# Loading the first block of input weights in two column halves, ahead of the buffer clears, in a two-layer decoder trunk

## What is computed

```python
def even_layer(h, w_in, conv_w, pool_w, pool_scale, w_out):
    xa, gb, gc, za, xp, zp = split(h @ w_in)              # six parts of 512 columns
    ya = short_gated_conv(xa, gb, gc, conv_w) * silu(za)  # gb * conv3(gc * xa)
    yb = multiscale_pool(xp, pool_w, pool_scale) * silu(zp)
    return concatenate([ya, yb], axis=-1) @ w_out

def odd_layer(h, w_in, ln_g, ln_b, w_s, b_s, w_out):
    u, v, z = split(h @ w_in, 3)                          # 1024 columns each
    v = layernorm(v, ln_g, ln_b)
    sv = tril(w_s) applied over chunks of 128 positions, per head, plus b_s
    return (u * sv * silu(z)) @ w_out

for i in range(2):
    h = rmsnorm(x, pre_norm[i])
    m = even_layer(h, ...) if i == 0 else odd_layer(h, ...)
    x = x + rmsnorm(m, post_norm[i])
```

## Time and profile before

| | us |
|---|---|
| median of 3 runs | 1076.64 |
| lowest, highest | 1073.21, 1088.56 |
| the profiled execution, its time | 1074.72 |
| its span on the slowest core (core 4) | 1073.2 |
| spans of the other seven | 1063.5 to 1069.7 |
| PE busy in the span | 978.3 |
| DVE, POOL, ACT busy | 691.9, 467.0, 385.5 |

### The profile page before, as it was taken

The page is one execution under the profiler, slowest core; times in us unless marked ns, Lnnn a source line. Parts: engine busy times, 40 slices in busy tenths (PEclk is TensorE's granted clock), DMA queues, the critical chain, the costliest instruction groups (busy, mean ns, idle before and its releaser), DMA issues.

```text
span 1073.2 us, 26957 instructions; the slowest of 8 cores (1063.5 to 1073.2 us)
## 1 busy us (share of the span) xinstructions
PE 978.3 (91%) x9144; PEld 857.3 (80%) x9144; DVE 691.9 (64%) x1826; ACT 385.5 (36%) x908; POOL 467.0 (44%) x703
## 2 busy tenths in 40 slices
PE   0879989999899999999999998999999999999994
PEld 0758878888788887878888887888888878887883
DVE  1565766658766664776666587666658657667651
ACT  3232524433433433343344234334432334324331
POOL 3223634454443545444344544434454444534452
PEclk9899999999999999999999999999999999999996
DMA  9999700222000022200002220000222000210011
GB/s 223 184 163 165 108 2 2 80 80 80 2 2 2 2 80 80 79 2 2 2 2 80 80 80 1 2 2 2 80 80 80 2 2 2 80 41 2 1 41 40
DMA packets 18328, 54.61 MB, mean 51 GB/s; under 512 B 1024, under 2 KB 1408, under 8 KB 18064
## 3 DMA queue, kind: packets, MB, share of 16 engines
q0 software_dynamic: 8592, 16.91, 10.5%
q1 hardware_dynamic: 9600, 35.98, 9.2%
HBM read 53.01 MB, written 16.78 MB: 65 GB/s over the span
## 4 chain that ended last, share of the span: by engine, by line
PE 62%; DVE 11%; POOL 8%; issue 7%; DMA 7%; ACT 4%; DVEq 0%; POOLq 0%; ACTq 0%; SPq 0%
PE psG L285 39%; PE psO L285 21%; DVE tmp L285 6%; POOL xres L285 5%; DMA Win<-win 4%; ACT tmp L285 2%; PE psT L285 2%; DVE small L285 2%; DMA xres<-x 2%; POOL small L285 2%; DMA out<-xres 1%; ACT xs L285 1%; DVE yT L285 1%; DVE pooled L285 1%; DVE hbuf L285 1%
## 5 line engine op out<-in xcount | busy, mean ns | idle before, releaser
L285 PE MATMUL psG<-hT,Win 128*128 128x256 bf16 x5120 | 602.7, 274 | 22.5 <-DVE yT L285 7.0
L285 PEld LDWEIGHTS psG<-hT,Win 128*128 128x128 bf16 x5120 | 493.1, 98 | 88.7 <-issue 30.5
L285 ACT ACTIVATE tmp<-psG 128x256 f32<-128x256 f32 (+1 forms) x324 | 121.8, 380 | 367.5 <-PE psG L285 201.3
L285 PE MATMUL psO<-Wout,yT 128*128 128x256 bf16 x2048 | 240.5, 276 | 12.4 <-DVE tmp L285 5.6
L285 PEld LDWEIGHTS psO<-Wout,yT 128*128 128x128 bf16 x2048 | 200.5, 99 | 39.5 <-issue 14.4
L285 POOL TENSOR_TENSOR yT<-tmp 128x256 bf16<-128x256 f32 x192 | 140.5, 734 | 198.6 <-DVE tmp L285 176.4
L285 POOL TENSOR_TENSOR xres<-xres,tmp 128x256 f32<-128x256 f32 x256 | 189.1, 739 | 81.6 <-DVE tmp L285 53.7
L285 POOL TENSOR_TENSOR small<-small,cstA 128x1 f32<-128x1 f32 x161 | 92.9, 581 | 241.4 <-DVE small L285 203.5
L285 ACT ACTIVATE tmp<-psO 128x512 bf16<-128x512 f32 x128 | 76.1, 594 | 142.4 <-PE psO L285 97.9
L285 DVE SCALAR_TENSOR_TENSOR tmp<-psG,cstA,cterm 128x128 f32<-128x128 f32 x256 | 89.0, 349 | 42.6 <-PE psG L285 25.2
L285 DVE SCALAR_TENSOR_TENSOR tmp<-psO,small,gpo_sb 128x256 f32<-128x256 f32 x256 | 106.9, 476 | 7.6 <-POOL small L285 6.0
(11 more groups left out here) (47 smaller groups left out, 680.0 us busy)
## 6 DMA issues: line engine op xcount, KB each, us to landing
xres<-x SPq DMA_DIRECT2D x16, 1024.0 KB, 5.3
out<-xres SPq DMA_DIRECT2D x16, 1024.0 KB, 4.1
Win<-win POOLq DMA_DIRECT2D x12, 1024.0 KB, 21.5
Wout<-wout POOLq DMA_DIRECT2D x4, 1024.0 KB, 19.0
gpo_sb<-gpo SPq DMA_DIRECT2D x1, 1024.0 KB, 23.3
cterm<-bsb SPq DMA_DIRECT2D x1, 512.0 KB, 16.8
xres<-wst SPq DMA_DIRECT2D x1, 512.0 KB, 19.5
tmp<-cst SPq DMA_DIRECT2D x1, 128.0 KB, 3.2
```

The source lines that it names most:

```text
L285: ins = getattr(e, name)(**kw)
```

## The change

The first block of layer 0 (`w00`, columns 0 to 1023) is loaded in two DMAs by columns instead of two by rows: columns 0 to 511 (chunks 0 to 3) on semaphore `w00`, and 512 to 1023 (chunks 4 to 7) on a new semaphore `w0h`. The matmuls of a chunk wait only for their half. Each half counts as a group of its own in `wgroups`, so the rule "two before" is counted from them. The loads are written ahead of the clearing of `small`, `hbuf` and `xpbuf` on POOL. On SP the loads of `cterm`, `wst` and `gpo` now wait until both halves have landed.

```diff
-        B_smallall = smallbuf("all")
-        S.op("pool", ("memset", dict(ap=small[:, :], constant=0.0)), writes=[B_smallall])
...
+        wfine = {l: {} for l in range(2)}
+        def wdma_raw(sem, out_ap, in_ap, toklist):
+            if not wgroups or wgroups[-1] is not toklist:
+                wgroups.append(toklist)
             gi = len(wgroups) - 1
             dep = list(wgroups[gi - 2]) if gi >= 2 else []
-            t = S.op("pool", ("dma_start", dict(out=out_ap, in_=in_ap)), sem=f"w{l}{grp}", inc=16, extra=dep)
-            wtok[l][grp].append(t)
+            t = S.op("pool", ("dma_start", dict(out=out_ap, in_=in_ap)), sem=sem, inc=16, extra=dep)
+            toklist.append(t)
...
+                if cb == 0 and l == layers[0] and not OPT["wfold"]:
+                    ha, hb = [], []
+                    wdma_raw(f"w{l}0", Win[l][:, :, 0:512], win_d[l][:, 0:512].rearrange("(k p) n -> p k n", p=128), ha)
+                    wdma_raw("w0h", Win[l][:, :, 512:1024], win_d[l][:, 512:1024].rearrange("(k p) n -> p k n", p=128), hb)
+                    wtok[l][cb] = ha + hb
+                    for p_ in range(4):
+                        wfine[l][p_] = ha
+                        wfine[l][4 + p_] = hb
+                    wready[l][cb] = wtok[l][cb]
+                    continue
...
         load_weights(layers[0])
+        B_smallall = smallbuf("all")
+        S.op("pool", ("memset", dict(ap=small[:, :], constant=0.0)), writes=[B_smallall])
...
             S.op("sp", ("dma_start", dict(out=cterm[:, :, :], in_=bsb_d.rearrange("p (h t) -> p h t", h=8))),
-                 writes=[B_cterm], sem="su2", inc=16)
+                 writes=[B_cterm], sem="su2", inc=16, extra=wready[layers[0]][0])
...
-            S.op("pe", calls, reads=[B_hT[s][0], B_hT[s][1]], writes=[dstB], extra=wready[l][p // 8])
+            S.op("pe", calls, reads=[B_hT[s][0], B_hT[s][1]], writes=[dstB], extra=wfine[l].get(p, wready[l][p // 8]))
```

More of the change, by code:

```diff
@@ L346, in build_nc @@
         sem_names = ["pe", "act", "dve", "pool", "ld0", "ld1", "ld2", "st0", "st1", "st2",
-                     "su0", "su1", "su2", "su3", "su4", "su5", "su6"] + [f"w{l}{g}" for l in range(2) for g in range(4)]
+                     "su0", "su1", "su2", "su3", "su4", "su5", "su6", "w0h"] + [f"w{l}{g}" for l in range(2) for g in range(4)]
         sems = {n: es.enter_context(nc.semaphore(n)) for n in sem_names}
@@ L428, in build_nc, with wdma @@
         cpos = {l: {n: p for p, n in enumerate(_chunk_order(l))} for l in range(2)}
-        def wdma(l, grp, out_ap, in_ap):
-            if not wgroups or wgroups[-1] is not wtok[l][grp]:
-                wgroups.append(wtok[l][grp])
+        wfine = {l: {} for l in range(2)}
+        def wdma_raw(sem, out_ap, in_ap, toklist):
+            if not wgroups or wgroups[-1] is not toklist:
+                wgroups.append(toklist)
             gi = len(wgroups) - 1
             dep = list(wgroups[gi - 2]) if gi >= 2 else []
-            t = S.op("pool", ("dma_start", dict(out=out_ap, in_=in_ap)), sem=f"w{l}{grp}", inc=16, extra=dep)
-            wtok[l][grp].append(t)
+            t = S.op("pool", ("dma_start", dict(out=out_ap, in_=in_ap)), sem=sem, inc=16, extra=dep)
+            toklist.append(t)
+        def wdma(l, grp, out_ap, in_ap):
+            wdma_raw(f"w{l}{grp}", out_ap, in_ap, wtok[l][grp])
         fold_rr = [0]
@@ L471, in build_nc @@
         load_weights(layers[0])
+        B_smallall = smallbuf("all")
+        S.op("pool", ("memset", dict(ap=small[:, :], constant=0.0)), writes=[B_smallall])
+        S.op("dve", ("reciprocal", dict(out=small[:, 128:192], in_=cst[:, 48:112])),
+             reads=[B_cst], writes=[B_rcnt, B_smallall])
+        small_init[0] = B_smallall.w
+        for j in range(4):
+            S.op("pool", ("memset", dict(ap=hbuf[j][:, :], constant=0.0)), writes=[B_h[j]])
+            S.op("pool", ("memset", dict(ap=xpbuf[j][:, :], constant=0.0)), writes=[B_xp[j]])
+        S.op("dve", ("tensor_copy", dict(out=identb[:, :], in_=identf)), reads=[B_c2], writes=[B_identb])
         if 1 in layers:
             S.op("sp", ("dma_start", dict(out=cterm[:, :, :], in_=bsb_d.rearrange("p (h t) -> p h t", h=8))),
-                 writes=[B_cterm], sem="su2", inc=16)
-            S.op("sp", ("dma_start", dict(out=wst_f, in_=wst_d[:, :, :])), writes=[B_wstf], sem="su3", inc=16)
+                 writes=[B_cterm], sem="su2", inc=16, extra=wready[layers[0]][0])
+            S.op("sp", ("dma_start", dict(out=wst_f, in_=wst_d[:, :, :])), writes=[B_wstf], sem="su3", inc=16, extra=wready[layers[0]][0])
         S.op("sp", ("dma_start", dict(out=gpo[:, :, :], in_=gpo_d.rearrange("p (l d) -> p l d", l=2))),
-             writes=[B_gpo], sem="su5", inc=16)
+             writes=[B_gpo], sem="su5", inc=16, extra=wready[layers[0]][0])
         if 1 in layers:
```

## The result

The median went from 1074.16 us (10 runs, 1071.49 to 1201.35) to 1089.58 us (10 runs, 1086.77 to 1103.44): 15.4 us more, a ratio of 1.0155, 95% [1.0118, 1.0191]. The forecast was 1090.0.

What follows compares the result with a forecast made beforehand. PE was taken as the bound from about 100 us, passing on any delay at the start. The profiled 1074.7 us plus 15.4 for DVE's delay behind POOL's wait, other terms 0, gave 1090.1; range 1080 to 1102.

Steps and rivals of the forecast that it cites:

- Byte sum and `w02`: DMA stream at the start: same bytes in another order, so `w02` lands at 63.8 us again.
- The bound of -5.0: `w02` could land earlier by the first 5 us' unused part (2.4) and tile 2's load (2.6), together -5.0 us.
- Smaller pieces: Halves of `w00` double its packets; time goes with bytes, so 0 us, or +13.4 if packets count.
- The packet-count rival: Packets, not bytes, set DMA time: `w02` lands at 77, total 1103.5 us; chance 10%.
- Early halves: Halves of `w00` land at 21.4 and 28.1 us; PE begins tile 1 of A0 at about 25, not 38.
- `wst`: `wst` lands at 40 us, `psG0` and `psG1` free at 49.5, A1's end about 58 instead of 54; all hidden.
- The wait that decides: POOL's `w10` issue waits for `w02`, holding convolution work; four `w01` chunks done at 74, not 59.36; DVE's +15.4 us taken.
- an edge of +1.2: PE's half-clock spell may return after about 10 us of idling: 0 to +1.2 us, taken as 0.
- The sum: Whole kernel: 1074.7 + 15.4 = 1090.1 us, own range 1085 to 1104; chance 78%.
- Whatever the start gains or loses is passed on to the end: PE bounds the kernel from about 100 us; no later slack can catch up a change at the start.
- The early start is kept: Rival: all moves with PE's first work, 38.16 to 25, so -13 us, 1062; chance 4%.
- Hidden: Rival: POOL's wait doesn't reach PE; `w01` and A1's end near 58 rule, 0 to +4 us, 1077; chance 8%.

Runs made afterwards that it cites:

- experiment 10: As 9, with `w01`'s issue on POOL moved ahead of three of the five `small` operations of the first tiles: 1078.79 us, ratio 1.0039.
- experiment 3: The changed kernel with SP's loads of `cterm`, `wst` and `gpo` not waiting, scheduler left free: 1072.02 us, ratio 1.0014.
- experiment 5: The changed kernel with POOL's issues of `w03` and layer 1's blocks put back at their places before the change: 1076.92 us, ratio 1.0015.
- experiment 1: The changed kernel with `w10`'s issue moved behind all of group A's convolution operations on POOL: 1085.88 us, ratio 1.0117.
- 2: The kernel before, with only `w03`'s and `w10`'s issues moved to the changed kernel's places around the first convolution operation: 1091.13 us, ratio 1.0173.
- 4: As experiment 3, with `w03`'s and `w10`'s issues moved back to the changed kernel's places on POOL: 1089.94 us, ratio 1.018.
- 6: The changed kernel with the weight-issue rule "three before" in place of "two before": 1109.44 us, ratio 1.0327.
- 8: As experiment 7, with tile 2 of x and `gpo` loaded only after `w01`: 1074.41 us, ratio 0.9989.
- 9: As 8, with `w10`'s issue moved behind two `small` operations on POOL: 1076.44 us, ratio 1.0002.
- experiment 7: As experiment 3, with the sums of `wst` in banks `psO0` and `psO1`: 1070.01 us, ratio 0.9962; repeated at 1070.41 us, ratio 0.9953.

## Why the prediction was right

*Byte sum and `w02`.* Forecast 63.8, measured 64.35: the order of the transfers changed, not their sum. The bound of -5.0 was not used: the stream got a gap of its own. `w01`'s issue stood behind the last `small` operation of the first tiles and went out at 23.9, 3.4 us after its condition (20.5), and the DMA share fell to 0.76 at 25 to 30. I hadn't forecast that gap; it is about 1.4 us of the engines' time (5 us at 0.76 in place of the 1.05 of the next window), and may be why the lower bound wasn't reached; that wasn't tried by itself, since experiment 10 moves PE's start too.

*Smaller pieces.* Taken as 0, upper bound 13.4; measured about 1 (the queue totals above), and experiment 3 has the halves and no loss. The packet-count rival falls. The value was right, but the reason that I gave for it was weak: q1's packets against q0's are plain transfers against converting ones, and no row before the change told bytes from packets in q0.

*Early halves.* 21.4 and 28.1 forecast, 20.5 and 26.4 measured. But PE began at 29.15, not 25. I had only asked when the weights were there. Tile 1 of x landed at about 19.2 beside them, and its norm and transposes ended with the last `hT` at 28.9.

*`wst`.* Landing 40.5 (40), `cterm` done at 49.7 (49.5), A1 done at 58.7 (58). Hidden by what follows, as forecast; once the cover is gone, in experiment 5, PE is about 5 us late at 60.

*The wait that decides.* The links up to the last came within 0.5 us:

| | forecast | core 3 |
|---|---|---|
| `w10` issued | 65.9 | 66.4 |
| first tap, tile 1 | 67.15 | 67.6 |
| `hbuf` of A1, tile 0 | 68.75 | 69.1 |
| four `w01` chunks done | 74 | 76.0 |

The last row is off by 2: I had two chunks go in the shadow of the wait and took nothing for the clock. The chunks all ran after 70.8, and the 32 matmuls of that row took 5.20 us where experiment 1 took 3.65, after a granted clock of 0.50 at 65 to 70. So this term, which I took as 0 with an edge of +1.2, is 1.55, above the edge.

By the Trainium skill (DMA: Bandwidth & Descriptors, Anatomy of one DMA) the wait of a DMA sits in the sequencer that issues it. The 13.34 us on POOL agree, and so do experiments 2, 4 and 10, where only what stands behind an issue changes.

*The sum.* +15.4 forecast, +15.4 between the medians; that it agrees to a tenth is chance. The last step before the sum has no row behind it: the rows give 71.55 - 55.14 = 16.4 for DVE, and I took 15.4. On core 3 that write of `hbuf` ended at 72.5 against 54.2 in the kernel before, 18.3 later, and the span is 17.9 longer; over the cores the first store came 18.4 later, and the core median rose by about 17. So for the cores the sum was 2 to 3 us short: 1.0 in that step, up to 1.0 in the links of the table, the rest because cores differ (the forecast was read from core 4, whose write ended at 55.1) and perhaps the clock. That the slowest core's median shows 15.4 and no more is luck; that the sum agrees within 2 or 3 us is the chain above. "Whatever the start gains or loses is passed on to the end" held for the losses (after, 10, and 6 with 3 us more) and for the gain of 3 (2.5 us at `w01`, 2.1 at the end). It failed for 8 and 9, which lead by 6 us at `w01` and at the first output projection, and end 2.4 and 1.3 us ahead of before.

*Rivals.* "The early start is kept" needed two things, POOL's issues elsewhere and `psG0` free; with both (experiment 7) the dense work starts 10 us earlier over the cores and the gain is 4 to 5 us, not 13: `w01`'s landing then decides when its chunks start, at 51.3. "Hidden" is what experiment 5 builds by hand: 1076.9, where I had worked out 1077.

## What to carry to other kernels

When a DMA issue that waits for an earlier transfer shares an engine with compute, list what stands between it and its condition: its price is, to a first estimate, the landing time less the moment at which the first needed operation behind it was ready, whatever is transferred. An edit elsewhere (here three waits on SP) can move such an issue when a scheduler makes the orders; so compare the order on every engine before and after, not only the edit. Removing one such wait can show the next one, as in experiment 1, so move all of them behind the work that is due, as in experiment 5, before judging the idea. And read a lead at several later moments and on all cores: in 9 the lead over 7 was still there at 90 us and gone at 195, and core 3 alone would have hidden this (its first store came at 191.3 in 9 and 194.0 in 7).

## What the runs showed of the hardware

- Pieces of 1 KB in place of 2 KB on the SBUF side, read from float32 and written as bf16, cost hardly anything: 9616 packets took 111 to 114 us of each engine's time on the eight cores of after, 8592 took 111 to 113 in the kernel before. By packet count it would have been 13.4 more. In experiments 7 to 10, with the halves and other orders, it was 113 to 116.
- Transfers of the SP queue and of POOL's queue share the engines at once, whichever was issued first: the two tiles of x, issued at 2.9 to 3.9 as before, took 13.4 us in the middle where they took 11.4, because the halves now start 2 us earlier beside them (core 3 of both), and the first half of `w00` landed over the cores at 20.2 with two tiles of x on SP beside it (after), at 24.0 to 24.2 with `cterm` and `wst` too (8, 9, 10), and at 25.1 with `gpo` as well (3).
- PE's clock: after 10.6 us of idleness the granted clock was 0.50 (the 1.2 GHz level) in the window from 65 to 70, and the 32 matmuls from 70.81 took 5.20 us instead of 3.65. After a short wait it went either way: in experiment 7 core 3 idled 2.77 us before `w01` and had 0.50 at 52 to 54, its 32 matmuls taking 5.00 us, while core 6 idled 3.03 us, kept 1.00 and took 3.65.
